# Attention: GpSimd multiplies the exponentials by the reciprocal of their sum, in place of VectorE

## The reference, cut to what matters

```
scale = (QK_NOPE_DIM + QK_ROPE_DIM) ** -0.5
def attend(blk):                       # one block of 128 queries, all 8 heads
    qn, qr = blk
    s = (jnp.einsum('bqhd,bkhd->bhqk', qn, k_nope)
         + jnp.einsum('bqhr,bkr->bhqk', qr, k_rope))
    p = jax.nn.softmax(s.astype(jnp.float32) * scale, axis=-1).astype(v.dtype)
    return jnp.einsum('bhqk,bkhd->bqhd', p, v)
```

## Time and profile before

| | |
|---|---|
| median of 3 runs | 2362.97 us (2356.22 to 2364.37) |
| the profiled execution, its own time | 2362.01 us |
| its span, first to last instruction | 2360.2 us |
| mean granted TensorE clock | 0.987 |
| busy PE, DVE, ACT, POOL | 2277.0, 1328.7, 937.6, 166.5 us |
| attention of the first layer | some 83 us, from 1281 to 1364 us of the span |

### The profile page before, as it was taken

One profiled execution on the slowest core, in us unless ns is written; L12 is line 12 of the kernel. 1 busy time (PEld: TensorE's weight loads), 2 busy tenths in 40 slices (PEclk: granted clock), 3 DMA queues, 4 the chain that ended last, 5 costly groups with the idle time before them and its releaser, 6 DMA issues.

```text
span 2360.2 us, 31189 instructions
## 1 busy us (share of the span) xinstructions
PE 2277.0 (96%) x12510; PEld 1827.7 (77%) x12510; DVE 1328.7 (56%) x2076; ACT 937.6 (40%) x1561; POOL 166.5 (7%) x150
## 2 busy tenths in 40 slices
PE   5999999988999999999999999999999999999998
PEld 4898886855887878888877578888888658888886
DVE  7677777786776354443456644344454654434445
ACT  3555555444326242332445543222244554222222
POOL 0000000000100100000223020000011302000001
PEclk8999999998999999999999999999999999999999
DMA  6344526632544222322321023232233102232232
GB/s 267 108 134 134 179 81 199 181 102 72 165 137 179 91 90 98 98 98 93 101 92 62 27 72 98 98 97 93 97 99 96 54 19 90 98 98 92 97 98 90
DMA packets 117248, 252.28 MB, mean 107 GB/s; under 512 B 45104, under 2 KB 49968, under 8 KB 116208
## 3 DMA queue, kind: packets, MB, share of 16 engines
q1 hardware_dynamic: 102816, 215.15, 27.9%
q0 software_dynamic: 5136, 18.88, 2.5%
q10 hardware_dynamic: 9152, 16.26, 2.1%
HBM read 225.07 MB, written 25.17 MB: 106 GB/s over the span
## 4 chain that ended last, share of the span: by engine, by line
PE 88%; DVE 5%; ACT 3%; DMA 1%; issue 1%; SPq 1%; POOL 0%; ACTq 0%; DVEq 0%; POOLq 0%
PE bank L1422 20%; PE bank L1424 20%; PE bank L1423 20%; PE bank L1036 8%; PE bank L1035 3%; PE bank L1607 2%; PE bank L1303 2%; PE bank L1620 1%; PE bank L1133 1%; PE bank L1134 1%; PE bank L1135 1%; DMA xt<-in_xt 1%; PE bank L1340 1%; PE bank L1649 1%; DVE smal L2909 1%
## 5 line engine op out<-in xcount | busy, mean ns | idle before, releaser
L1952 ACT ACTIVATE whi<-raw 128x1024 fp32r<-128x1024 f32 (+1 forms) x268 | 278.9, 1041 | 900.7 <-PE bank L1424 897.5
L1422 PE MATMUL bank<-ahi,whi 128*128 128x512 f32 x1152 | 452.7, 393 | 4.8 <-DVE alo L2775 3.8
L1423 PE MATMUL bank<-alo,whi 128*128 128x512 f32 x1152 | 449.0, 390 | 0.0
L1424 PE MATMUL bank<-ahi,wlo 128*128 128x512 f32 x1152 | 449.0, 390 | 0.0
L2661 DVE TENSOR_TENSOR wlo<-raw,whi 128x1024 fp32r<-128x1024 f32 (+1 forms) x268 | 325.0, 1213 | 138.2 <-ACT whi L1952 138.1
L1422 PE MATMUL bank<-bhi,whi 128*128 128x512 f32 x736 | 286.5, 389 | 0.0
L1424 PE MATMUL bank<-bhi,wlo 128*128 128x512 f32 x736 | 286.3, 389 | 0.0
L1423 PE MATMUL bank<-blo,whi 128*128 128x512 f32 x736 | 286.3, 389 | 0.0
L1422 PEld LDWEIGHTS bank<-ahi,whi 128*128 128x128 f32 x1152 | 216.7, 188 | 53.8 <-issue 6.6
L1423 PEld LDWEIGHTS bank<-alo,whi 128*128 128x128 f32 x1152 | 216.9, 188 | 45.7 <-issue 1.4
L1424 PEld LDWEIGHTS bank<-ahi,wlo 128*128 128x128 f32 x1152 | 216.7, 188 | 45.3
(11 more groups left out here) (437 smaller groups left out, 3608.8 us busy)
## 6 DMA issues: line engine op xcount, KB each, us to landing
raw<-in_s_gu SPq DMA_DIRECT2D x88, 512.0 KB, 3.2
raw<-in_s_qkvx SPq DMA_DIRECT2D x34, 512.0 KB, 3.5
late_modw<-in_w_mod POOLq DMA_DIRECT2D x32, 512.0 KB, 3.8
raw<-in_s_up SPq DMA_DIRECT2D x32, 512.0 KB, 3.3
raw<-in_s_down SPq DMA_DIRECT2D x32, 512.0 KB, 3.2
raw<-in_s_dn SPq DMA_DIRECT2D x32, 512.0 KB, 3.3
raw<-in_s_win SPq DMA_DIRECT2D x24, 512.0 KB, 3.3
raw<-in_s_zg SPq DMA_DIRECT2D x16, 512.0 KB, 3.5
```

The costliest lines, as they stand in the source:

```text
L1422: pe.matmul(out, w_hi, x_hi, start=start, stop=False)
L1423: pe.matmul(out, w_hi, x_lo, start=False, stop=False)
L1424: return pe.matmul(out, w_lo, x_hi, start=False, stop=stop)
L1952: act.activation(whi[u % 2][:, 0:width[u + 2] * P], raw[u % 2][:, 0:width[u + 2] * P], ACT.Identity).then_inc(hi_ready, 1)
```

## The change

The multiplication by the reciprocal moves from DVE to GpSimd, 32 operations in each layer. DVE's reciprocal raises `pn_ready`, GpSimd waits for it, multiplies `eb[m % 3]` in place, and raises `pool_done`; PE's transposes wait on `pool_done` in place of `pn_ready`. `scaled_rows(l, m)` is the count that `pool_done` has behind tile m of layer l. DVE no longer waits on its own reciprocal (`after`).

```
+        def scaled_rows(l, m):
+
+            return (15 + 4 * MH) * l + 15 + m + 1
...
-                    pe.wait_ge(pn_ready, pn_ready_0 + m0 + m + 1)
+                    pe.wait_ge(pool_done, scaled_rows(l, m))
...
                     dve.wait_ge(e_ready, e_ready_0 + m0 + m + 1)
-                    after(dve.reciprocal(smal[:, 6 + m % 3:7 + m % 3], smal[:, 3 + m % 3:4 + m % 3]))
-                    dve.tensor_scalar(eb[m % 3][:, :], eb[m % 3][:, :], smal[:, 6 + m % 3:7 + m % 3], None, ALU.mult).then_inc(pn_ready, 1)
+                    dve.reciprocal(smal[:, 6 + m % 3:7 + m % 3], smal[:, 3 + m % 3:4 + m % 3]).then_inc(pn_ready, 1)
...
+                for m in range(4 * MH):
+                    pool.wait_ge(pn_ready, pn_ready_0 + 4 * MH * l + m + 1)
+                    pool.tensor_scalar(eb[m % 3][:, :], eb[m % 3][:, :], smal[:, 6 + m % 3:7 + m % 3], None, ALU.mult).then_inc(pool_done, 1)
+                    n_pool[0] += 1
+                    assert n_pool[0] == scaled_rows(l, m)
                 group(2 + 2 * l)
```

## The result

The changed kernel takes 2393.66 us in the median of 4 runs (2390.09 to 2396.41), the kernel before 2363.35 (2356.22 to 2364.37, 4 runs). The ratio is 1.0132, with 95% between 1.0115 and 1.0149: slower by 30.3 us, where I had forecast 9. The profiled execution took 2390.09.

A forecast was written before the change was run, and what follows sets the result against it. The prediction took TensorE, busy for 96% of the span, to bound the kernel. Waits at its transposes, 4.5 us per layer, added 9.0 to 2363.0, with nothing for VectorE's relief: 2372 us, range 2363 to 2390.

The forecast's parts named there:

- X: Time of one scaling multiplication on GpSimd, taken as 0.90 us between its copy's 0.61 and its two-tile product's 1.27.
- d: Delay of a late tile's transposes with the scaling on GpSimd: X + 0.12 - 0.59 = X - 0.47, forecast 0.43 us.
- the prediction's own formula: Attention loss per layer: 11 d - 0.24 + 7 (d - 0.5), last term only if positive; 9.0 us for two layers.
- Delays add: Each late tile lengthens TensorE's own order and the next maximum waits for its scores, so the tiles' delays were summed.
- The places: Tiles that pay in a layer: 11 tight ones about d each, seven with 0.5 us slack the excess, 14 nothing.
- 11 times or a little more: How often TensorE's matmuls at the transposes would wait for GpSimd in a layer, about 5 + 4.7 us.
- The late loop: Two tiles of the attention's late loop would take 4.23 + 0.39 = 4.6 us, a growth of d - 0.04.
- The hops: Hand-overs from VectorE's reciprocal to GpSimd and from GpSimd to TensorE's transposes, 0.06 us each.
- VectorE's relief, costed at nothing: VectorE loses 31 us of scalings, but its maxima wait for TensorE's scores, so no gain was counted.
- The ports: Rival: VectorE and GpSimd block each other; 10 splits and low parts at 0.9 us each add 9.0 us, giving 2381.
- blocked, or above 1.40: Rival: the engines block each other or one GpSimd multiplication exceeds 1.40 us; slower, chance 0.11.
- Nearly hidden: Rival: GpSimd multiplies about as fast as it copies, 0.61 to 0.80 us; 2365.6 to 2369.8 us, chance 0.22.

The follow-up runs named there:

- e2_imm: The changed kernel with GpSimd multiplying by the constant 0.5 in place of the column of reciprocals: 2389.39 us, ratio 1.0109 to the kernel before.
- e3_two: The changed kernel with GpSimd multiplying each tile by itself, a product of two tiles: 2376.54 us, ratio 1.0058 to the kernel before.
- e7_early: The changed kernel with the reciprocal of an even tile issued ahead of the next tile's maximum on VectorE: 2378.24 us, ratio 1.0063 to the kernel before.
- e6_extra: The kernel before, with an additional GpSimd tile-by-column multiplication of another tile beside each VectorE scaling: 2362.56 us, ratio 1.0008.
- e1_copy: The changed kernel with GpSimd copying each tile onto itself in place of multiplying, same order and waits: 2364.31 us, ratio 1.0008 to the kernel before.
- e4_odd: Half of the change: GpSimd multiplies the odd tiles, VectorE the even ones as before: 2372.95 us, ratio 1.0054 to the kernel before.
- e11_column: The changed kernel with the same multiplication written as a product of two tiles, the second repeating the column: 2377.51 us, ratio 1.0064 to the kernel before.
- e5_even: The other half of the change: GpSimd multiplies the even tiles, VectorE the odd ones: 2392.11 us, ratio 1.0125 to the kernel before.

## Why the prediction was wrong, step by step

**The step that failed: X.** "I see nothing that would bring it under the copy, so the ends are 0.61 and 1.27, and I take 0.90" is where it went wrong. The operation takes 1.562 us, above both ends. I took the nearest rows, GpSimd's copy and its product of two tiles, for bounds; they were two other operations. The argument by traffic (one tile in and one out, as in the copy) is refuted by e2_imm, which has the copy's traffic and takes 1.491, and by e3_two, which reads the tile twice and takes 1.041. The page that I cited beside it, the Trainium skill, GPSIMD Engine Reference, section Performance versus the Vector engine (roughly twice as slow as VectorE; its measured row is an addition of two tiles, 1.96 times), was nearer with 0.97 and still far below the 3.2 times measured. The same page's rule on operations with one input, section When to use GPSIMD, held for the copy (0.617) and not for the multiplication.

With the measured hops, d is X + 0.10 + 0.05 - 0.59 = X - 0.44, and X = 1.562 gives d = 1.12. Put into the prediction's own formula that is 2 (12.3 - 0.24 + 4.3) = 32.8 us; the runs give 30.3, and 31.4 in the attention, of which about 28 is waiting. So most of the miss is this term.

**A second step that failed: "Delays add".** With d = X - 0.44 the formula has 3.4 us for the growth of the attention at 0.617 (2.1 measured), 14.1 at 1.041 (13.5 and 13.4), 30.4 at 1.491 (26.3, without a stretch at half clock) and 32.8 at 1.562 (28 without the clock). It is within 1.5 us where d is small and 4 to 5 us high where d is large. The places themselves were right; what fails is that a late odd tile and the even one behind it were both counted. Tiles 4, 6, 18 and 20 stand behind tiles 3, 5, 17 and 19, and in the first layer the formula has 0.62 for the first and 1.12 for each of the others, 4.0 us, where they pay 0.05, 0.13, 0.38 and 0.47, 1.0 us. That is 6 us too much in two layers. Some 2 us of it come back, mostly since tiles 3, 11, 13 and 17 pay 0.75 and tile 5 1.03 in place of 0.62. So the 32.8 comes near the 31.4 of the attention partly by luck: it is some 5 us too high in the waits and has none of the 3 us of clock. TensorE's matmuls waited 17 times in the first layer and not "11 times or a little more": with d at 1.1 six of the seven tiles with a slack of 0.3 to 0.6 wait too, and tile 4 is covered by tile 3's wait. Tile 28 stays the odd one out that the earlier trace rows showed.

**The late loop.** "Wrong in the places if the period grows by another amount than d - 0.04": it grew by 1.02, where d - 0.04 is 1.08. e7_early takes this loss away without touching the duration.

**The hops.** 0.06 and 0.06 forecast, 0.10 and 0.05 measured.

**VectorE's relief, costed at nothing.** Right: the idle time of the maxima rose from 27.5 to 57.5 us, all of it ended by TensorE's scores.

**The ports.** The price of the multiplication is its own and not that of blocking. The maxima stayed at 0.69. The splits in the attention and the low part of the first mix, two inputs from SBUF each, read as follows in the first layer:

```profile
L2927 DVE TENSOR_TENSOR blo<-rt,bhi 128x512 fp32r<-128x512 f32 x2 | 1.6, 796 | 0.0
L2665 DVE TENSOR_TENSOR wlo<-raw,whi 128x1024 fp32r<-128x1024 f32 x2 | 2.4, 1216 | 0.0
```

The low part has gone from a mean of 0.68 to 0.80 us (one of the two, the one that lies wholly inside a multiplication of GpSimd's, took 0.91), the splits are where they were. For the splits this says little, since none of them meets a multiplication on GpSimd here; the one at 1332.63 in e6_extra, which does, takes 0.3 us longer. That is some tenths of a microsecond and not the 9 us of that rival. The rule that I cited for it, the Trainium skill, SBUF — State Buffer, section "Summary: rules for kernel authors", would have the later of the two instructions wait for the whole of the earlier in e6_extra, if VectorE's scaling counts as one in a two-port mode, and so would it for the split with its two SBUF inputs. The trace doesn't agree: 0.54 us inside a multiplication of 1.6 for the scaling, 1.53 in place of 1.22 for the split.

**A step that was missing: the clock.** I had no term for it. No window of the attention before shows less than the full clock, and the change brings stretches of 3.4 and 6.8 us at half clock behind waits of TensorE of about 2 us, some 3 us of the 31.4. What sets them off stays open. The kernels without such a stretch (e1_copy, e2_imm, e4_odd, e7_early, e11_column) still show the rest, so the waits are the main cause and this one is added to them.

**The rivals.** Nearest came "blocked, or above 1.40", with a chance of 0.11, for its second half. "Nearly hidden" (0.22) took X up to 0.80; of the forms that ran on GpSimd only the copy is there, and it multiplies nothing. The range ended at 2390 because I had let the rate of another operation, 1.27 with some room up to 1.40, end it.

## What to carry to other kernels

An instruction that the trace of this engine doesn't show isn't bounded by its neighbours: the same multiplication took 0.49 us on VectorE and 1.56 or 1.04 on GpSimd depending on how it was written, so measure the form, or keep the range open upward. Before handing work to another engine to relieve one that waits, look at what the waiting instruction holds back behind it: moving the reciprocals and the copies ahead of it won 11.7 us here with no engine changed. Where two waits of the bounding engine follow each other, look at what was issued ahead of the first: what goes on during it makes the second shorter, and the two delays don't add. And where that engine is made to wait in new places, look at its granted clock as well as at the waits.

## What the runs showed of the hardware that I had not expected

- GpSimd, 128x512 f32: copy 0.617 us, a tile times itself or times a repeated column 1.041, a product of two different tiles 1.269, a tile times a constant 1.491, a tile times a column as a scalar operand 1.562. Why the scalar form is 1.5 times the tile form, and why two different tiles take longer than one tile and a column, stays open.
- TensorE's granted clock falls to half for 3.4 us, or twice that, behind some of its waits of about 2 us, and not behind others: e2_imm, with 26.3 us more in the attention, has none, and e5_even, with 32.8, has six of them. What decides it these runs don't show.
- VectorE's tile-by-column multiplication beside GpSimd's (e6_extra): 12 of 64 take 0.72 to 0.911 us in place of 0.487, and 28 of GpSimd's 64 take 1.61 to 2.184 in place of 1.567.
